# Four-product plain fp32 on 32-column tiles instead of split fp32r products, in a two-layer encoder kernel

## What is computed

```
hn   = rmsnorm(h, mix_norm_pre);  proj = hn @ w_in           # 1024 -> 2048: u, q, k, v
mix  = concat(pool_mixer(u), neighbourhood_attention(q, k, v)) @ w_out   # 1024 -> 1024
h    = h + rmsnorm(mix, mix_norm_post);  hn = rmsnorm(h, ffn_norm_pre)
f    = (silu(hn @ wg) * (hn @ wu)) @ wd       # layer 0: dense, 1024 -> 4096 -> 1024
f    = top-2-of-8 experts, each 1024 -> 3584 -> 1024         # layer 1
h    = h + rmsnorm(f, ffn_norm_post)
```

## Time and profile before

| | |
|---|---|
| median of 3 runs | 1309.68 us |
| profiled execution: its span, first to last instruction | 1308.4 us |
| mixing 0, from first product to the norm of token tile 0 | 12.5 to 97.9 us |
| dense, same borders | 110.9 to 369.4 us |
| mixing 1, same borders | 382.3 to 464.8 us |
| experts, from first product to the last | 489 to 1295 us |
| PE, PEld, DVE, ACT, POOL busy | 98%, 61%, 31%, 22%, 8% |
| data moved | 443.50 MB; 193 GB/s in the dense part, 425 GB/s in the experts |

### The profile page before, as it was taken

How to read it: one execution, slowest core, us unless ns; L and a number is a source line. 1 busy time by engine, 2 the same in 40 slices (tenths; PEclk the granted TensorE clock), 3 DMA queues, 4 the chain that set the end, 5 groups by cost and what they waited for, 6 DMA issues and landing times.

```text
span 1308.4 us, 31062 instructions
## 1 busy us (share of the span) xinstructions
PE 1285.0 (98%) x14397; PEld 794.5 (61%) x14397; DVE 409.0 (31%) x565; ACT 286.0 (22%) x433; POOL 108.4 (8%) x240
## 2 busy tenths in 40 slices
PE   9999999999999999999999999999999999999996
PEld 8888999999989863354353364345353355336443
DVE  6886555555567850030210120030030031021011
ACT  4666344444466630000000000000000000000101
POOL 3334200000000307300000000000000000000000
PEclk9999999999999989999999999999999999999999
DMA  9646855555543399999999999999999999999994
GB/s 303 221 175 211 259 193 193 193 193 193 193 158 141 146 425 427 425 421 398 427 424 426 426 424 425 425 425 425 425 424 425 425 426 424 425 426 424 426 425 187
DMA packets 67012, 443.50 MB, mean 339 GB/s; under 512 B 4520, under 2 KB 10800, under 8 KB 42304
## 3 DMA queue, kind: packets, MB, share of 16 engines
q1 hardware_dynamic: 64736, 433.58, 81.4%
q0 software_dynamic: 2144, 7.90, 2.1%
HBM read 439.36 MB, written 2.10 MB: 337 GB/s over the span
## 4 chain that ended last, share of the span: by engine, by line
PE 90%; DMA 4%; DVE 2%; ACT 1%; SPq 1%; issue 1%; ACTq 0%; DVEq 0%
PE psum L1077 38%; PE psum L1086 18%; PE psum L730 9%; PE psum L732 9%; PE psum L731 9%; DMA unit<-in_moe_w_down 3%; PE psum L1021 2%; PE psum L1032 1%; PE psum L827 1%; DMA ring<-in_w_in 1%; PE psum L818 1%; SPq L385 1%; PE psum L844 1%; ACT pt L1230 1%; PE psum L759 1%
## 5 line engine op out<-in xcount | busy, mean ns | idle before, releaser
L1077 PE MATMUL psum<-unit,xT 128*32 128x448 f32 x5376 | 507.0, 539 | 0.1
L1077 PEld LDWEIGHTS psum<-unit,xT 128*32 128x32 f32 x5376 | 174.9, 110 | 326.9 <-issue 324.8
L1086 PE MATMUL psum<-unit,hid 128*32 128x256 f32 x4704 | 259.1, 380 | 2.4 <-DMA unit<-in_moe_w_down 2.4
L1086 PEld LDWEIGHTS psum<-unit,hid 128*32 128x32 f32 x4704 | 152.0, 110 | 107.0 <-issue 5.3
L1744 DVE TENSOR_TENSOR hidp<-hid,psum 128x448 f32<-128x448 f32 x42 | 38.4, 915 | 535.4 <-PE psum L1077 535.4
L1424 DVE TENSOR_TENSOR w_lo<-ring,w_hi 128x2048 fp32r<-128x2048 f32 x64 | 149.9, 2350 | 112.8 <-ACT w_hi L1189 112.5
L730 PE MATMUL psum<-hT_hi,w_hi 128*128 128x256 f32 x656 | 183.3, 279 | 0.1
L732 PE MATMUL psum<-hT_hi,w_lo 128*128 128x256 f32 x656 | 182.1, 278 | 0.0
L731 PE MATMUL psum<-hT_lo,w_hi 128*128 128x256 f32 x656 | 182.1, 278 | 0.0
L1189 ACT ACTIVATE w_hi<-ring 128x2048 fp32r<-128x2048 f32 x71 | 135.1, 1910 | 59.2 <-PE psum L732 53.0
L730 PEld LDWEIGHTS psum<-hT_hi,w_hi 128*128 128x128 f32 x656 | 123.2, 188 | 2.0 <-issue 1.4
(11 more groups left out here) (253 smaller groups left out, 947.9 us busy)
## 6 DMA issues: line engine op xcount, KB each, us to landing
unit<-in_moe_w_gate SPq DMA_DIRECT2D x64, 1792.0 KB, 31.8
unit<-in_moe_w_up SPq DMA_DIRECT2D x64, 1792.0 KB, 26.3
unit<-in_moe_w_down SPq DMA_DIRECT2D x64, 1792.0 KB, 31.2
ring<-in_dense_w_gate SPq DMA_DIRECT2D x8, 2048.0 KB, 9.1
ring<-in_dense_w_up SPq DMA_DIRECT2D x8, 2048.0 KB, 9.0
ring<-in_dense_w_down SPq DMA_DIRECT2D x8, 2048.0 KB, 8.2
ring<-in_w_in SPq DMA_DIRECT2D x6, 2048.0 KB, 8.7
ring<-in_w_out SPq DMA_DIRECT2D x4, 2048.0 KB, 8.8
```

Source lines behind the costliest of these rows:

```text
L1077: ins = mm(bank(half, s)[quad(j)], xT[:, s, dt, :], w[:, at:at + FJ], start=dt == 0, stop=dt == DT - 1)
L1086: ins = mm(down_out[s][quad(j)], e[:, half, s, t, :], w, start=half == t == 0 and s != 2, stop=half == 1 and t == FT - 1, skip_group_check ...
```

## The change

**Products.** `product` becomes four matmuls, one for each 32 columns of the stationary operand, on unsplit fp32. `w_hi`, `w_lo`, all lo copies, and their instructions on ACT and DVE go (`split_to`, `split_part`, `dhid_hi`/`dhid_lo`, `yaT_hi`/`yaT_lo`, `ypT_hi`/`ypT_lo`, `hT_hi`/`hT_lo`; `open_half`). `hT` is filled by `tokens_low` on ACT and `tokens_high` on DVE.

```
-                mm(dst, still[0], moving[0], start=start, stop=False)
-                mm(dst, still[0], moving[1], start=False, stop=False)
-                return mm(dst, still[1], moving[0], start=False, stop=stop)
+                for j in range(4):
+                    ins = mm(dst[quad(j)], still[:, quad(j)], moving, start=start, stop=stop)
+                return ins
```

**PE's order in `mixing`.** Turns stand elsewhere:

```
-                for g in range(GROUPS):
-                    if g < 7:
-                        scores(g + 1)
-                    fill(4 + g // 2, g % 2)
-                    if g == 7:
-                        values(2)
-                    turn(g)
-                    if g in (3, 4):
-                        values(g - 3)
+                whole(0)
+                whole(2)
+                fill(1, 0)
+                scores(0)
+                fill(1, 1)
+                fill(3, 0)
+                scores(1)
+                fill(3, 1)
...
+                turn(0)
+                fill(4, 0)
+                scores(2)
+                fill(4, 1)
+                turn(1)
+                fill(5, 0)
+                scores(3)
+                fill(5, 1)
+                turn(2)
+                values(0)
+                fill(6, 0)
+                scores(4)
+                turn(3)
+                fill(6, 1)
+                scores(5)
+                turn(4)
+                values(1)
+                fill(7, 0)
+                scores(6)
+                turn(5)
+                fill(7, 1)
+                scores(7)
+                turn(6)
+                values(2)
+                turn(7)
```

**DVE's order in `mixing`**, and the bias of layer 0, whose half b = 0 moves from GpSimd to DVE:

```
+                def first_bias(quarter):
+                    dve.wait_ge(rwords_landed[0][quarter], 64)
+                    bias_step(dve, 0, quarter, 0).then_inc(bias_first, 1)
...
+                    first_bias(0)
+                fill(2, kT[:, 0:2, :])
+                if layer == 0:
+                    first_bias(1)
+                add_bias(0)
+                fill(3, kT[:, 2:4, :])
+                if layer == 0:
+                    first_bias(2)
+                    first_bias(3)
+                add_bias(1)
+                normalise(0)
+                for g in range(2, GROUPS):
+                    if g == 3:
+                        fill(4, vv[:, :, 0:C2])
+                    if g == 7:
+                        fill(7, uT[:, 2:4, POOL_PAD:POOL_PAD + S])
                     add_bias(g)
-                    split_part(h0 + 5 + g // 2, g % 2)
-                    normalise(g)
...
+                    normalise(g - 1)
+                normalise(7)
```

```
-RING = 3
-STAGE = 3
+RING = 4
+EARLY_UNITS = (6, 12, 18)
...
-                    sp.wait_ge(split_ready, 2 * (seq - RING) + 2)
+                    sp.wait_ge(half_done, halves_done(seq - RING))
...
+                if j in EARLY_UNITS:
+                    load_unit(0, zeroth, EARLY_UNITS.index(j))
+            load_mixing(1, 0)
             sp.wait_ge(scored, GROUPS * DEPTH)
...
+            load_unit(0, zeroth, 3)
+            load_unit(0, zeroth, 4)
             sp.wait_ge(pv_done, GROUPS * DEPTH)
             sp.wait_ge(delta_ready, 3 * DEPTH)
...
+            load_unit(0, zeroth, 5)
+            load_unit(0, zeroth, 6)
+            sp.wait_ge(half_done, halves_done(MOE0 - 2))
+            load_unit(0, zeroth, 7)
+            sp.wait_ge(half_done, halves_done(MOE0 - 1))
+            load_unit(0, zeroth, 8)
+            sp.wait_ge(delta_dve_ready, DEPTH)
             load_unit(0, zeroth, 9)
+            load_unit(0, zeroth, 10)
```

More of the change, by code:

```diff
@@ L9 @@
 F32 = mybir.dt.float32
-F32R = mybir.dt.float32r
 I32 = mybir.dt.int32
@@ L74 @@
 DENSE = ffn_order(DBLOCKS)
-FILL_ENGINE = (0, 1, 0, 0, 0, 1, 0, 1)
+FILL_ORDER = (0, 2, 1, 3, 4, 5, 6, 7)
+FILL_ENGINE = (0, 0, 1, 1, 1, 0, 0, 1)
 FILLS = (FILL_ENGINE.count(0), FILL_ENGINE.count(1))
+FILL_PLACE = [FILL_ORDER.index(f) for f in range(8)]
 UNITS = 3 * DT
@@ L83 @@
 N_UNITS = NE * UNITS
-SLOT_OF = [n % SLOTS for n in range(N_UNITS - 2)] + [SLOTS - 1, 0]
+SLOT_OF = [n % SLOTS for n in range(N_UNITS - 1)] + [0]
 assert N_UNITS % SLOTS == 0 and H_SLOT not in SLOT_OF[N_UNITS - SLOTS + H_SLOT:]
@@ L200, in hybrid_encoder @@
         spread = sb("spread", [P, NT, TG, P], over="gpre")
-        units = [sb(f"unit{k}", [P, UNIT], over="bias", skip=4 * UNIT * k) for k in range(SLOTS)]
+        units = [sb(f"unit{k}", [P, UNIT], over="early", skip=4 * UNIT * k) for k in range(SLOTS)]
         ident = cst[:, K_ID:K_ID + P]
@@ L241, in pt, with by_columns, by_rows, halves_done @@
             return t[:, k % 2, :].rearrange("p (k m q) -> p k m q", k=2, m=4)
[L243 to L264, removed]
+        def by_columns(seq, c):
+            return ring[:, seq % RING, :].rearrange("p (t n) -> p t n", t=DT)[:, :, c * C2:(c + 1) * C2]
+        def by_rows(seq, c):
+            return ring[:, seq % RING, c * 8 * C2:(c + 1) * 8 * C2].rearrange("p (t n) -> p t n", t=2)
+        def halves_done(seq):
+            at = seq - mixing_first_load(seq // (MIX_LOADS + DENSE_LOADS))
+            if at < 4:
+                return 2 * (seq - at) + max(FILL_PLACE[2 * at], FILL_PLACE[2 * at + 1]) + 1
+            return 2 * seq + 2
         psum = ctx.enter_context(nc.psum_tensor("psum", [P, 8 * C4], F32))
@@ L365, in wait_fill @@
             n = FILL_ENGINE[f]
-            eng.wait_ge((fill_act, fill_dve)[n], FILLS[n] * layer + FILL_ENGINE[:f + 1].count(n))
+            sofar = [FILL_ENGINE[g] for g in FILL_ORDER[:FILL_PLACE[f] + 1]].count(n)
+            eng.wait_ge((fill_act, fill_dve)[n], FILLS[n] * layer + sofar)
         def word_buffer(layer, quarter):
@@ L385, in load_rwords, with bias_step @@
                 eng.dma_start(dst, src).then_inc(rwords_landed[layer][quarter], 16)
+        def bias_step(eng, layer, quarter, b):
+            at = word_buffer(layer, quarter)[:, 8 - 8 * b:]
+            words = bass.AP(at.tensor, at.offset,
+                            [list(at.ap[0]), [RPB_H if layer else SEEN, 4], [RPB_R, ROWS], [1, WIN]])
+            m = mask[:, b, :].unsqueeze(1).unsqueeze(1).broadcast_to([P, 4, ROWS, WIN])
+            first = 8 * (quarter // 2) + quarter % 2
+            return eng.tensor_tensor(biasv[:, first:first + 7:2, b], words, m, ALU.add)
         def window_delta(eng, link, layer, g, bufs):
@@ L474, in by_tile, with part_of @@
             def by_tile(w):
                 return w.rearrange("(t p) n -> p t n", p=P)
[L477 to L481, removed]
+            def part_of(layer, j):
+                c = (1, 2, 3, 0)[j]
+                return by_tile(w_in[layer])[:, :, c * C4:(c + 1) * C4]
@@ L482, in _, with load_mixing @@
+            def load_mixing(layer, first):
+                s0, wo = mixing_first_load(layer), by_tile(w_out[layer])
+                for j in range(first, 4):
+                    load(s0 + j, part_of(layer, j), DT)
                 load(s0 + 4, wo[:, 4:8, :], 4)
                 load(s0 + 5, wo[:, 0:4, :], 4)
[L484 to L491, removed]
@@ L504, in _ @@
             zeroth = slice(0, 1)
+            load_part(0, 0, part_of(0, 0), half_landed[0])
+            load_rwords(sp, 0, 0)
+            sp.dma_start(cst[:, P:K_ALL], consts[:, P:K_ALL]).then_inc(cst_landed, 16)
+            load_part(1, 0, part_of(0, 1), half_landed[1])
+            load_rwords(sp, 0, 1)
+            load_part(0, 1, part_of(0, 0), w_landed[0])
+            load_part(1, 1, part_of(0, 1), w_landed[1])
+            load_rwords(sp, 0, 2)
+            load_rwords(sp, 0, 3)
+            load_mixing(0, 2)
+            for j, (what, b) in enumerate(DENSE):
+                cut = slice(b * C4, (b + 1) * C4)
+                if what == "down":
+                    load(MIX_LOADS + j, by_tile(d_down[0, cut]), 4)
+                else:
+                    w = d_gate if what == "gate" else d_up
+                    load(MIX_LOADS + j, by_tile(w[0])[:, :, cut], DT)
+                if j in EARLY_UNITS:
+                    load_unit(0, zeroth, EARLY_UNITS.index(j))
+            load_mixing(1, 0)
             sp.wait_ge(scored, GROUPS * DEPTH)
-            load_unit(0, zeroth, 0)
-            sp.wait_ge(delta_dve_ready, DEPTH)
-            load_unit(0, zeroth, 1)
+            load_unit(0, zeroth, 3)
+            load_unit(0, zeroth, 4)
             sp.wait_ge(pv_done, GROUPS * DEPTH)
             sp.wait_ge(delta_ready, 3 * DEPTH)
[L511 to L517, removed]
+            load_unit(0, zeroth, 5)
[5 more added lines that the diff above has]
+            sp.wait_ge(delta_dve_ready, DEPTH)
             load_unit(0, zeroth, 9)
+            load_unit(0, zeroth, 10)
             sp.wait_ge(h_parked, 16 * NT)
             sp.wait_ge(hs_ready, 2 * 4)
-            load_unit(0, zeroth, 10)
             sp.wait_ge(logits_done, 1)
@@ L572, in build_bias @@
                     pool.wait_ge(rwords_landed[layer][quarter], 64)
[L573 to L576, removed]
-                        m = mask[:, b, :].unsqueeze(1).unsqueeze(1).broadcast_to([P, 4, ROWS, WIN])
```

(29 more changed lines are left out.)

420 lines of the change are left out of this document (127 added, 293 removed).

## The result

The changed kernel takes 1458.60 us (median of 4 runs, 1457.55 to 1459.66), against 1309.66 us for the one before on the same chip (1309.25 to 1310.13). The ratio is 1.1132, with a 95% interval of 1.1117 to 1.1148: 11.3% slower. The prediction said 1441 us, with a range of 1408 to 1464 us. Its profiled execution has a span of 1457.8 us, 149.4 us more than before; the sum of the prediction was 131.6.

A forecast was written before the change was run, and what follows sets the result against it. PE's products were taken as the bound. Mixing 0 +31.7, dense +68.7, mixing 1 +33.6 and experts -2.4 made 131.6 us on the 1308.4 us span, 1440.0, plus 1.3 for the median: 1441 us, range 1408 to 1464 (own range 1428 to 1452).

The forecast's parts named there:

- rival 1: Mixing, both layers: DVE's chain stays hidden and the turns do not wait; 1406.5 us, chance 0.12.
- rival 2: Mixing: the granted clock falls in the new PE waits, costing 15 to 34 us; about 1466 us, chance 0.13.
- The bound: Stages before the experts: PE's products set the time, not splits or DMA; freed DVE work gives nothing back.
- The price of the product: All changed products: 0.4318 us against 0.3405 for 256 columns, 0.858 against 0.686 for 512.
- the shared moving columns: New product: four tiles stream the same moving columns, unlike the experts; no row shows this, no difference was assumed.
- The dense stage: Dense part between the mixing layers: dearer products add 68.7 us, 1.4 of it beside the next norm.
- The waits before the turns: Mixing: PE waits for DVE's chain before turn(0), turn(3) to turn(6) and turn(7); 18.1 us in layer 0, 16.4 in layer 1.
- The switches: Mixing: about ten added changes between matmul forms, 0.11 us each, 1.1 us a layer, between 0 and 2.2.
- The clock: Mixing: the summed forecast had no term for a fall of the granted clock during PE's waits.
- The experts: Expert stage: units loaded early remove the down projections' DMA waits, saving 2.4 us.
- rival 3: All stages: four tiles overlap so a 256-column product takes 0.216 us; 1196 us in all, chance 0.03.
- rival 4: Experts: DMA takes the lead and some units come late, 4.3 us each; 1445 to 1450 us, chance 0.04.

The follow-up runs named there:

- experiment 5: The kernel of experiment 1 with fill(4, 0) also moved ahead of turn(0): 1409.37 us, ratio 1.0765 to the kernel before.
- experiment 6: The kernel before, splits, order, buffers and loads kept, but each product four plain fp32 matmuls on 32-column tiles of the high parts (output incomplete): 1408.84 us.
- experiment 3: The changed kernel with each product as one plain fp32 128x128 matmul in place of four on 32-column tiles: 1458.07 us, ratio 1.1138.
- experiment 2: The changed kernel with seven to eleven plain fp32 products on idle data before turn(0) and turn(3) to turn(6): 1440.58 us.
- experiment 4: The changed kernel without early loads, units 0 to 2 loaded after the last scores of mixing 1: 1458.48 us, ratio 1.1127.
- experiment 1: The changed kernel with scores(4) to scores(7) each moved ahead of a half fill, and DVE's fill(7) behind normalise(6): 1419.11 us.

## Why the prediction was right or wrong

**The range** of 1408 to 1464 us holds the measured 1458.60 us, but the forecast's own range of 1428 to 1452 does not. The wide range was drawn to take in part of rivals 1 and 2, and it held because rival 2 came true, which the prediction thought unlikely.

**The bound** was read rightly. PE's products limited the stages before the experts, and DVE's and ACT's work lay beside them: half of it went and nothing was won (experiments 5 and 6).

**The price of the product** held. The dense part has 4096 + 1024 records in 331.12 us; 512 x 0.4318 + 128 x 0.858 = 330.9 us. It was read from the expert rows, with the one open point of the shared moving columns, and experiment 3 closes it.

**The dense stage** grew by 66.4 us instead of 68.7. The timelines show where the 2.3 us are, first before, then after:

```profile
374.42 0.40 PE L732 MATMUL psum<-w_hi,dhid_lo 128*128 128x512 f32 x1
...
375.19 1.28 DVE L1511 TENSOR_TENSOR hs<-psum,gpost 128x512 f32<-128x512 f32 x2
```

```profile
481.02 0.68 DVE L1404 TENSOR_TENSOR hs<-psum,gpost 128x512 f32<-128x512 f32 x1
```

Before, the last product starts at 374.42 us, so with its pace of 0.23 us the products took 263.7 us from 110.92 on, 1.6 us more than the paces of the earlier trace rows give (512 x 0.3405 + 128 x 0.686 = 262.1); after, they took only 0.2 us more than the sum. The loss per product was right, and the base from which it was counted was 1.4 us too short. The other 0.9 us are at the border: from the end of the products to the next first one it took 382.30 - 374.65 = 7.65 us before and 6.7 after. The last eight products now last 6.9 us instead of 5.5, and DVE does the first half of tile 1's multiply beside them, at 481.02, which it did behind them before.

**The waits before the turns** came out in place and, in sum, in size: 17.7 and 16.1 us against 18.1 and 16.4. The single ones differ more: `turn(0)` waited 5.0 us in layer 0 and 3.5 in layer 1 (5.6 and 3.9 foreseen), `turn(3)` to `turn(6)` 2.9, 3.7, 2.9 and 3.2 us in both (3.05 each), and `turn(7)` not at all (0.3). The bias add on DVE, taken as 0.85 us for want of a row, took 0.74 us in the chain (two in 1.47 us).

**The switches** were priced at 1.1 us a layer, but the sum carries 3.7 us for old and new ones, which is what was left over for the old ones and small waits alone, so the new ones are not in it. Half a fill takes 3.59 us in the chain behind scores or a turn and 3.45 behind `values`, so a switch costs 0.14 us, near the 0.11 foreseen.

**The clock** is the step that failed. The forecast left the granted clock at 1.00 and made its fall a rival with a chance of 0.13, for the reason that a fill of 3.45 us at full load stands in each cycle. That reason was wrong: the clock fell all the same, behind every one of the ten long waits, for 23.5 and 20 us, and this cost 18.0 us (experiment 2). The forecast missed by 17.6 us, so this one term, put at nothing, is the size of the whole miss. Rival 2 gave 15 to 34 us for it and 1466 us in all; the measured time lies nearer to that than to the forecast. The rule of the Trainium skill (TensorE: Matmul & The Clock Gate, Why this matters for your kernels), which warns against idle gaps between bursts, stood beside that rival, and the trace agrees with it. I had the gap, its size and a fall in routing in the rows before, and a chance of 0.13 was too low for that.

**The experts** lose 1.1 us instead of winning 2.4. The failed step is that units which lie ready take away the last waits for DMA. Those waits became longer, 3.5 us against 2.4. The early units are not the cause: the waits are 4.2 us without them (experiment 4) and 3.4 us in experiment 6, which has the old loads. Experiment 4 shows why the lead does not reach the end. Why the end waits for 1 us more stays open.

**Rivals 1, 3 and 4.** The turns did wait, and taking the waits away gave 49 us, more than their length (experiments 1 and 5). A product of half the price is excluded by the dense stage and experiment 3. The DMA in the experts moved the time by no more than 1.1 us.

No version here beats the kernel before. The products alone cost 100 us of PE time, and nothing else on the path is of that size.

## What to carry to other kernels

A split into three fp32r products beats plain fp32 here, 0.3405 us against 0.4318 for 256 columns, as long as the splits lie on engines with time to spare: freeing those engines is worth nothing when PE is the bound. When products get dearer or the order changes, look at what stands between a result and its next use on PE; here four calls moved on PE, and one on DVE, were worth 39 us. And count an idle wait of PE at more than its length, since the granted clock can fall behind it; if the wait cannot be removed, products on idle data in it are worth trying.

## What the runs showed of the hardware that was not expected

- Waits of 2.9 to 5.0 us, with scores and transposes next to them, lowered the granted clock to its half level each of ten times, even though 3.5 us or more of full products ran between one wait and the next. Seven to eleven products on idle data in each wait kept it at 1.00, worth 18.0 us. In experiment 5 the clock still fell once, for 3.4 us from 47.9 us on, 1.9 us behind the end of a wait of only 1.5 us.
- DVE's four multiplies (L1473) last 0.94 us as a rule but 1.71 us before `turn(4)`, in both layers of the changed kernel. Its timeline in layer 0:

```profile
84.82 1.71 DVE L1473 TENSOR_SCALAR prob_b<-prob_b,rinv 128x160 f32<-128x160 f32 x4
84.90 0.72 POOL L389 TENSOR_TENSOR delta<-win_a,uT 128x256 f32<-128x256 f32 x1
...
85.70 0.73 POOL L381 TENSOR_TENSOR win_a<-uT 128x271 f32<-128x271 f32 x1
```

  GpSimd's window sums run beside them. The kept traces bear this out: of the 512 such multiplies in all eight, the 385 that overlap a GpSimd instruction by 0.02 us at most each lasted 0.31 us or less, while 68 of the other 127 lasted over 0.33 us. No run was made to try it alone.
